# Moving rows of a hybrid decoder step's projections, begun at other bytes modulo 64

## The chip, the cores and the metric

The kernel runs on one NeuronCore of a Trainium2 chip. The metric is the device time of one execution in microseconds. The kernel before was timed twice: 1699.39 and 1699.59 us, median 1699.49 us. A profile of one further execution, and the packed trace of it, are what is read below.

## What is computed

One layer of a decoder, over a prompt of 256 tokens with 16 learned tokens ahead of it, and 8 sample sequences of one token each, 280 token columns in all. Model width 2048, feed-forward width 5632 (up-projection 11264). Cut to what matters:

```
z   = rmsnorm(x) @ w_in                       # 2048 -> 128 strips of 128 features, and 16 for the gates
mix = sigmoid(g_a)*shortconv_branch + sigmoid(g_b)*mlstm_branch
x   = x + mix @ w_out                         # 2048 -> 2048
up  = causal_dwconv(rmsnorm(x) @ w_up)        # 2048 -> 11264
x   = x + (silu(up[5632:]) * up[:5632]) @ w_down   # 5632 -> 2048
y   = rmsnorm(x)[16:]                         # and the states
```

Everything is float32, and the products must keep nearly that precision.

## The kernel before, in words

Tokens lie along the free dimension, features along the 128 partitions. Every large projection is a loop over strips of 128 output features. A strip takes KT = 16 blocks of the contraction (FC = 22 for each half of the last projection), in units of 8 (KU), the last one of 6. For a unit, 8 blocks of weights are fetched by the SP queue into `w_raw` (a ring of RING = 4 slots of 4096 bytes in a partition), ScalarE writes their high part as fp32r to `w_hi` (L712), VectorE the rest to `w_lo` (L985), and TensorE multiplies three times, in `unit`: high weights by the high part of the activations (L1524), high weights by the low part (L1528), low weights by the high part (L1532), 8 matmuls each. Each matmul has a 128x128 stationary operand of its own; the moving operand is one row of an activation tile, 264 to 280 fp32r numbers. All of them run into one PSUM bank, and the next strip goes to the next of four banks.

The activations are held as a high and a low tile:

- `xh`, `xl`: 16 rows of 280 numbers, 1120 bytes from row to row. Strips of the first projection read columns 12 to 279 (268, C0 = 12) or, for three of each head's sixteen, 0 to 279 (280). The sums for the gates (`gates`, L1475) read 280 with a stationary operand of 104 columns.
- `mh`, `ml`: 16 rows, 1088 bytes from row to row (MW = 272), 266 numbers from column MX = 4. Input of the out-projection.
- `x2h`, `x2l`: the same form, in the memory of `xh` and `xl`. Input of the up-projection.
- `hh`, `hl`: 22 rows of 264 numbers, 1056 bytes from row to row, input of the last projection.

The allocation puts `x_parts` (and so `xh` and `xl`) at a multiple of 64 bytes, `x2h`, `x2l`, `mh`, `ml`, `hh` and `hl` at 32 above one, and the three weight rings at multiples of 64. The first number that a matmul reads of a row thus lies, modulo 64 bytes, at

| rows | numbers | before, even/odd row | changed, even/odd row |
|---|---|---|---|
| xh, column 12 on | 268 | 48 / 16 | 56 / 24 |
| xl, column 12 on | 268 | 48 / 16 | 28 / 60 |
| xh, column 0 on | 280 | 0 / 32 | 8 / 40 |
| xl, column 0 on | 280 | 0 / 32 | 44 / 12 |
| mh, ml | 266 | 48, 48 | 56, 52 |
| x2h, x2l | 266 | 48, 48 | 0, 60 |
| hh | 264 | 32 / 0 | 48 / 16 |
| hl | 264 | 32 / 0 | 56 / 24 |

Other fp32r matmuls are untouched. Among them is the state sum of `back` (L1619 to L1622), whose moving rows are 258 numbers of `v_hi` and `v_lo`: the first block's at 32 (`v_hi`) and 0 (`v_lo`), the second block's at 40 and 8, since these rows are 1032 bytes apart, the third block's (`v_hi` alone) at 48.

The tiles are written once each by ScalarE (L731) and VectorE (L1027 for `xl`, L1246 and L1249 for `mh` and `ml`, L1281 and L1284 for `x2h` and `x2l`, L1340 and L1342 for `hh` and `hl`).

What the diff touches, with the lines of the profile:

Of the kernel before, what the change touches and what calls it, by code (L numbers as in the profile page):

```python
# [6 lines left out]
def hybrid_decoder_step(nc, ins, outs, scratch_rows, scratch_v, scratch_q):  # L7
# [10 lines left out]
    f32, f32r = mybir.dt.float32, mybir.dt.float32r  # L18
    ALU, ACT = mybir.AluOpType, mybir.ActivationFunctionType
# [7 lines left out]
    P = 128  # L27
# [9 lines left out]
    KT = D // P  # L37
    FT = DFF // P
    TP = NMETA + SEQ
    NT = TP + NS  # L40
# [4 lines left out]
    NM = NT - M0  # L45
    PM = TP - M0
    NF = NT - NMETA
    MX = 4
    MW = (MX + NM + 7) // 8 * 8
    T2 = TP - 2 * P  # L50
    TL = NT - 2 * P
# [14 lines left out]
    KU = 8  # L66
# [37 lines left out]
    with ctx:  # L104
        def sb(name, shape, dt=f32):
            return ctx.enter_context(nc.sbuf_tensor(name, shape, dt))
# [4 lines left out]

        xres = sb("xres", [P, KT, NT])
        x_parts = (nc.sbuf_base + 31) // 32 * 32
        sb("x_parts", [P, 2 * KT * NT])
        xh = nc.alloc_sbuf_tensor_at("xh", [P, KT, NT], f32r, offset=x_parts)
        xl = nc.alloc_sbuf_tensor_at("xl", [P, KT, NT], f32r, offset=x_parts + KT * NT * 4)
        x2h = nc.alloc_sbuf_tensor_at("x2h", [P, KT, MW], f32r, offset=x_parts + 32)
        x2l = nc.alloc_sbuf_tensor_at("x2l", [P, KT, MW], f32r, offset=x_parts + 32 + KT * NT * 4)
        w_raw = sb("w_raw", [P, RING, KU * P])
        w_hi = sb("w_hi", [P, RING, KU * P], f32r)  # L120
        w_lo = sb("w_lo", [P, RING, KU * P], f32r)
# [25 lines left out]
        def at(name, shape, dt=f32):  # L147
            size = int(np.prod(shape[1:])) * 4
            size = (size + 31) // 32 * 32
            t = nc.alloc_sbuf_tensor_at(name, shape, dt, offset=base + cursor[0])  # L150
            cursor[0] += size
            assert cursor[0] <= REGION, (name, cursor[0])
            return t
# [126 lines left out]
        wfx = at("wfx", [P, WR // Q + 1, Q])  # L280
        hh_end = cursor[0]
        cursor[0] = 0
        hl = at("hl", [P, FC, NF], f32r)
        cursor[0] = hh_b
        hh = at("hh", [P, FC, NF], f32r)
        assert hh_end <= cursor[0]
        yt = at("yt", [P, 2, D])
        cursor[0] = FC * NF * 4
        ys = at("ys", [P, P])
        xs = at("xs", [P, KT, NS])  # L290
        x3 = at("x3", [P, 2, NF])
# [76 lines left out]
        def col(c, j):  # L368
            return vecs[:, bass.ds(c * KT + j, 1)]
# [612 lines left out]
        def _(v):  # L982
# [144 lines left out]
            def back(n):  # L1127
# [6 lines left out]
                for i in range(8, HEAD_U):  # L1134
# [89 lines left out]
                    for jj in range(2):  # L1224
                        j = n * 2 + jj
                        k = i - 12 * jj
                        if k == 12:

                            v.wait_ge(cu_done, j + 1)
                            v.tensor_scalar(cv[:, :], cu[:, 2:NCU], col(5, j), None, ALU.mult).then_inc(conv_step, 1)  # L1230
                            v.wait_ge(conv_step, j * 5 + 1)
                            v.scalar_tensor_tensor(out=cv[:, 0:PM], in0=cu[:, 1:1 + PM], scalar=col(4, j), in1=cv[:, 0:PM],
                                                   op0=ALU.mult, op1=ALU.add).then_inc(conv_step, 1)
                        if k == 13:
                            v.wait_ge(pre_step, 3)
                            v.tensor_tensor(cv[:, PM:NM], cv[:, PM:NM], pre_s[:, bass.ds(j, 1), :].rearrange("p a b -> p (a b)"),
                                            ALU.add).then_inc(conv_step, 1)
                            v.wait_ge(conv_step, j * 5 + 2)
                            v.scalar_tensor_tensor(out=cv[:, 0:PM], in0=cu[:, 0:PM], scalar=col(3, j), in1=cv[:, 0:PM],
                                                   op0=ALU.mult, op1=ALU.add).then_inc(conv_step, 1)  # L1240
                        if k == 14:
                            v.tensor_scalar(cu_last[:, :, bass.ds(j, 1)].rearrange("p t a -> p (t a)"), cu[:, NCU - NLAST:NCU],
                                            1.0, None, ALU.mult).then_inc(conv_step, 1)
                        if (k == 26 and jj == 0) or (k == 19 and jj == 1):
                            v.wait_ge(mixed, j + 1)
                            v.tensor_scalar(mh[:, bass.ds(j, 1), MX:MX + NM].rearrange("p a t -> p (a t)"), mx[:, :], 1.0, None,  # L1246
                                            ALU.mult).then_inc(mix_split, 1)
                            v.wait_ge(mix_split, j * 2 + 1)
                            v.tensor_tensor(ml[:, bass.ds(j, 1), MX:MX + NM].rearrange("p a t -> p (a t)"), mx[:, :],  # L1249
                                            mh[:, bass.ds(j, 1), MX:MX + NM].rearrange("p a t -> p (a t)").bitcast(f32),  # L1250
                                            ALU.subtract).then_inc(mix_split, 1)

            front(0, first=True)
# [5 lines left out]
            def tile_of(t, m, a, b):  # L1259
                return t[:, bass.ds(m, 1), a:b].rearrange("p a t -> p (a t)")  # L1260
# [10 lines left out]
            def out_four(n):  # L1271
                for q in range(4):
                    m = n * 4 + q
                    step(n, 8, U_B, 2 * q)
                    v.wait_ge(unit_used, used(n * 8 + (U_B + 2 * q + 1)))
                    v.wait_ge(sq_done, m + 1)
                    v.wait_ge(x2g_step, m * 2 + 1)
                    v.tensor_tensor(x2s[:, :], bank[q][:, 0:NM], tile_of(xres, m, M0, NT), ALU.add)\
                     .then_inc(evacuated, 1)
                    v.wait_ge(evacuated, out_of(n * 4 + (S_B + q)))  # L1280
                    v.tensor_scalar(tile_of(x2h, m, MX, MX + NM), x2s[:, :], col(1, m), None, ALU.mult).then_inc(x2g_step, 1)  # L1281
                    v.tensor_scalar(tile_of(xres, m, M0, NT), x2s[:, :], 1.0, None, ALU.mult)
                    v.wait_ge(x2g_step, m * 2 + 2)
                    v.scalar_tensor_tensor(out=tile_of(x2l, m, MX, MX + NM), in0=x2s[:, :], scalar=col(1, m),  # L1284
                                           in1=tile_of(x2h, m, MX, MX + NM).bitcast(f32), op0=ALU.mult,
                                           op1=ALU.subtract).then_inc(x2g_step, 1)
                    step(n, 8, U_B, 2 * q + 1)

# [115 lines left out]
        def _(pe):  # L1404
# [107 lines left out]
                turn(aux[2][:, t * P:(t + 1) * P], sc_rows[:, t, :], P)  # L1512
            turn(aux[2][:, 2 * P:2 * P + NS * H], n_rows[:, :], NS * H).then_inc(f_turned, 1)

            def unit(u, slot, b, k0, kk, rh, rl, c0, c1, first, last, waits=(), frees=1):


                pe.wait_ge(hi_done, u + 1)
                for k in range(kk):
                    for at_k, sm, value in waits:  # L1520
                        if at_k == k:
                            pe.wait_ge(sm, value)
                    w = slice(k * P, (k + 1) * P)
                    pe.matmul(bank[b][:, 0:c1 - c0], w_hi[:, slot, w], rh[:, k0 + k, c0:c1],  # L1524
                              start=(first and k == 0), stop=False)
                for k in range(kk):
                    w = slice(k * P, (k + 1) * P)
                    pe.matmul(bank[b][:, 0:c1 - c0], w_hi[:, slot, w], rl[:, k0 + k, c0:c1], start=False, stop=False)  # L1528
                pe.wait_ge(lo_done, u + 1 + RING)
                for k in range(kk):  # L1530
                    w = slice(k * P, (k + 1) * P)
                    mm = pe.matmul(bank[b][:, 0:c1 - c0], w_lo[:, slot, w], rh[:, k0 + k, c0:c1],  # L1532
                                   start=False, stop=(last and k == kk - 1))
                if frees:
                    mm.then_inc(unit_used, frees)

            def strip(s, u, i, b, rh, rl, c0, c1, need=(), between=None):

                for h in range(2):
                    if h == 1 and between is not None:
                        between()
                    waits = [(k - h * KU, sm, x) for k, sm, x in need if k // KU == h]
                    if h == 1:
                        waits.append((2, evacuated, s + 2))
                    unit(u + h, (i + h) % RING, b, h * KU, KU, rh, rl, c0, c1, h == 0, h == 1, waits)

            def tiles_ready(done, per, start, n):

# [92 lines left out]
            back(H - 1)  # L1643

            def out_strip(i, q, need=()):
                strip(i * 4 + (S_B + q), i * 8 + (U_B + 2 * q), 2 * q, q, mh, ml, MX, MX + NM, need)

            def out_unit(q, h, waits, frees):
                unit(U_B + 2 * q + h, 2 * q + h, q, h * KU, KU, mh, ml, MX, MX + NM, h == 0, h == 1, waits, frees)

            out_unit(0, 0, ((0, mix_split, KT),), 1)
            out_unit(1, 0, ((0, evacuated, S_B + 2),), 0)
# [6 lines left out]
                    out_strip(i, q)  # L1659

            def up_strip(c, i, q, need=(), between=None):
                strip(i * 4 + (S_C + c * S_CH + q), i * 8 + (U_C + c * U_CH + 2 * q), 2 * q, q, x2h, x2l, MX, MX + NM, need, between)

            def down_strip(c, i, q, need=(), bank_free=None):

# [96 lines left out]
```

## Time and profile before

| what | value |
|---|---|
| median of two timed executions | 1699.49 us |
| the profiled execution | 1699.21 us |
| its span, first to last instruction | 1697.5 us |
| mean granted TensorE clock | 0.998 |
| TensorE busy with matmuls | 1686.0 us, 99% |
| VectorE, ScalarE, GpSimd busy | 70%, 45%, 28% |
| HBM traffic | 187 GB/s over the span |

A group of matmuls in the profile shows the mean time of one from its start to its end. Matmuls overlap, so that mean (some 285 ns) is not what one costs. What one costs is the distance between starts. In the timeline, a row gives the start of the first of a run of equal instructions and their number; the distance between the starts of two rows, divided by the matmuls between them, is the cost of one.

### The profile page before, as it was taken

How to read it: one execution, taken by the hardware profiler on the slowest of the kernel's cores; microseconds unless marked ns; L12 is line 12 of the kernel's file. 1: busy time of each engine (PE TensorE's matmuls, PEld its weight loads, DVE VectorE, ACT ScalarE, POOL GpSimd, SP SyncE). 2: the span in 40 equal slices, each digit the busy share in tenths (PEclk: the TensorE clock that was granted, in tenths of full speed). 3: DMA queues.
4: the chain of work that ended last, by engine and by line, in shares of the span. 5: the costliest groups of instructions: out<-in, count | busy, mean ns of one | idle time of the engine just before them, and what ended most of it. 6: DMA issues, size and time to landing. Idle time of an engine off the chain costs nothing.

```text
span 1697.5 us, 37171 instructions
## 1 busy us (share of the span) xinstructions
PE 1686.0 (99%) x13712; PEld 1679.5 (99%) x13712; DVE 1193.6 (70%) x1901; ACT 767.4 (45%) x916; POOL 477.9 (28%) x501
## 2 busy tenths in 40 slices
PE   9999999999999999999999999999999999999997
PEld 8999999999999999999999999999999999999997
DVE  5875857677585767758688877777545777777554
ACT  6545345354543535344445554544443433334443
POOL 4522415242241524224333222221000222222220
PEclk9999999999999999999999999999999999999999
DMA  8788786868778687887866666666666666666663
GB/s 212 187 227 196 202 214 166 216 176 216 190 195 213 174 210 178 216 195 190 193 176 187 188 178 180 184 174 178 184 179 183 181 180 177 180 180 177 184 177 120
DMA packets 591309, 318.80 MB, mean 188 GB/s; under 512 B 17756, under 2 KB 586060, under 8 KB 589156
## 3 DMA queue, kind: packets, MB, share of 16 engines
q1 hardware_dynamic: 578564, 292.99, 64.2%
q10 hardware_dynamic: 10592, 21.57, 5.1%
q0 software_dynamic: 2064, 2.92, 0.8%
q8 instruction: 72, 1.18, 0.3%
q14 instruction: 17, 0.14, 0.0%
HBM read 305.09 MB, written 12.78 MB: 187 GB/s over the span
## 4 chain that ended last, share of the span: by engine, by line
PE 99%; ACT 0%; DVE 0%; POOL 0%; issue 0%; ACTq 0%; POOLq 0%; DVEq 0%
PE strip L1524 32%; PE strip L1532 32%; PE strip L1528 32%; PE aux L1406 1%; PE strip L1455 0%; PE aux L1585 0%; PE aux L1414 0%; PE aux L1475 0%; PE strip L1468 0%; PE aux L1615 0%; PE aux L1614 0%; PE aux L1628 0%; PE strip L1406 0%; PE aux L1619 0%; PE aux L1620 0%; PE aux L1612 0%
## 5 line engine op out<-in xcount | busy, mean ns | idle before, releaser
L712 ACT ACTIVATE w_hi<-w_raw 128x1024 fp32r<-128x1024 f32 x557 | 588.7, 1060 | 787.7 <-PE strip L1532 768.8
L985 DVE TENSOR_TENSOR w_lo<-w_raw,w_hi 128x1024 fp32r<-128x1024 f32 x556 | 708.4, 1278 | 297.5 <-ACT w_hi L712 297.0
L1524 PE MATMUL strip<-xh,w_hi 128*128 128x268 f32 (+1 forms) x2016 | 290.9, 286 | 0.0
L1528 PE MATMUL strip<-xl,w_hi 128*128 128x268 f32 (+1 forms) x2016 | 290.0, 286 | 0.0
L1532 PE MATMUL strip<-xh,w_lo 128*128 128x268 f32 (+1 forms) x2016 | 290.0, 286 | 0.0
L1524 PEld LDWEIGHTS strip<-xh,w_hi 128*128 128x128 f32 x2016 | 265.1, 188 | 0.2
L1532 PEld LDWEIGHTS strip<-xh,w_lo 128*128 128x128 f32 x2016 | 265.2, 188 | 0.0
L1528 PEld LDWEIGHTS strip<-xl,w_hi 128*128 128x128 f32 x2016 | 265.2, 188 | 0.0
L1524 PE MATMUL strip<-x2h,w_hi 128*128 128x266 f32 x1408 | 200.1, 284 | 0.0
L1528 PE MATMUL strip<-x2l,w_hi 128*128 128x266 f32 x1408 | 199.9, 284 | 0.0
L1532 PE MATMUL strip<-x2h,w_lo 128*128 128x266 f32 x1408 | 199.8, 284 | 0.0
L1524 PEld LDWEIGHTS strip<-x2h,w_hi 128*128 128x128 f32 x1408 | 183.2, 189 | 0.1
L1532 PEld LDWEIGHTS strip<-x2h,w_lo 128*128 128x128 f32 x1408 | 183.2, 189 | 0.0
L1528 PEld LDWEIGHTS strip<-x2l,w_hi 128*128 128x128 f32 x1408 | 183.2, 189 | 0.0
L683 POOL TENSOR_TENSOR gg<-sg,cz 128x264 f32<-128x264 f32 x44 | 57.9, 1317 | 409.3 <-ACT sg L930 409.3
L686 POOL TENSOR_TENSOR hid<-gg,cz 128x264 f32<-128x264 f32 x44 | 73.7, 1674 | 101.7 <-DVE cz L1334 101.7
L1524 PE MATMUL strip<-hh,w_hi 128*128 128x264 f32 x704 | 102.2, 286 | 0.0
L1532 PE MATMUL strip<-hh,w_lo 128*128 128x264 f32 x704 | 101.3, 285 | 0.0
L1528 PE MATMUL strip<-hl,w_hi 128*128 128x264 f32 x704 | 101.2, 284 | 0.0
L1532 PEld LDWEIGHTS strip<-hh,w_lo 128*128 128x128 f32 x704 | 92.2, 189 | 0.0
L1528 PEld LDWEIGHTS strip<-hl,w_hi 128*128 128x128 f32 x704 | 91.9, 188 | 0.0
L1524 PEld LDWEIGHTS strip<-hh,w_hi 128*128 128x128 f32 x704 | 91.7, 188 | 0.0
(330 smaller groups left out, 1526.4 us busy)
## 6 DMA issues: line engine op xcount, KB each, us to landing
w_raw<-in_w_in SPq DMA_DIRECT2D x256, 512.0 KB, 4.5
w_raw<-in_w_up SPq DMA_DIRECT2D x176, 512.0 KB, 4.1
w_raw<-in_w_down SPq DMA_DIRECT2D x64, 512.0 KB, 3.9
w_raw<-in_w_out SPq DMA_DIRECT2D x32, 512.0 KB, 4.4
w_raw<-in_w_down SPq DMA_DIRECT2D x32, 384.0 KB, 3.3
out<-c_st ACTq DMA_DIRECT2D x8, 1024.0 KB, 7.1
c_st<-in_state_mlstm_C ACTq DMA_DIRECT2D x7, 1024.0 KB, 10.6
rb<-scratch_rows ACTq DMA_DIRECT2D x8, 270.0 KB, 5.3
```

What stands on the lines that cost most here:

```text
L683: g.tensor_tensor(gg[:, :], sg[:, :], cz[:, 0, :], ALU.mult).then_inc(gg_done, 1)
L686: g.tensor_tensor(hid[:, :], gg[:, :], cz[:, 1, :], ALU.mult).then_inc(hid_done, 1)
L712: act.activation(w_hi[:, slot, :], w_raw[:, slot, :], ACT.Copy).then_inc(hi_done, 1)
L985: v.tensor_tensor(w_lo[:, slot, :], w_raw[:, slot, :], w_hi[:, slot, :].bitcast(f32), ALU.subtract).then_inc(lo_done, 1)
L1406: return pe.transpose(out, in_, ident[0:k, 0:k])
L1524: pe.matmul(bank[b][:, 0:c1 - c0], w_hi[:, slot, w], rh[:, k0 + k, c0:c1], start=(first and k == 0), stop=False)
L1528: pe.matmul(bank[b][:, 0:c1 - c0], w_hi[:, slot, w], rl[:, k0 + k, c0:c1], start=False, stop=False)
L1532: mm = pe.matmul(bank[b][:, 0:c1 - c0], w_lo[:, slot, w], rh[:, k0 + k, c0:c1], start=False, stop=(last and k == kk - 1))
```

## The change

Constants for where each tile's rows begin take the place of the common ones. The flat tiles get 8 or 16 numbers more, and a shifted view of the flat tile is the tile. `mh` and `ml` keep their places and are used from column 6 and 5 on in place of 4; `unit` and `strip` get an argument `l0`, the first column in the low tile.

```diff
-    MX = 4
+    MX, MH, ML = 4, 6, 5
+    X2H, X2L, HS, HL, XH, XL = 8, 15, 4, 6, 2, 3
...
-        sb("x_parts", [P, 2 * KT * NT])
-        xh = nc.alloc_sbuf_tensor_at("xh", [P, KT, NT], f32r, offset=x_parts)
-        xl = nc.alloc_sbuf_tensor_at("xl", [P, KT, NT], f32r, offset=x_parts + KT * NT * 4)
-        x2h = nc.alloc_sbuf_tensor_at("x2h", [P, KT, MW], f32r, offset=x_parts + 32)
-        x2l = nc.alloc_sbuf_tensor_at("x2l", [P, KT, MW], f32r, offset=x_parts + 32 + KT * NT * 4)
+        sb("x_parts", [P, 2 * KT * NT + 16])
+        def rows_from(flat, shift, n, width):
+            return flat[:, shift:shift + n * width].rearrange("p (k t) -> p k t", t=width)
+
+        xh = rows_from(nc.alloc_sbuf_tensor_at("xh", [P, KT * NT + 8], f32r, offset=x_parts), XH, KT, NT)
+        xl = rows_from(nc.alloc_sbuf_tensor_at("xl", [P, KT * NT + 8], f32r, offset=x_parts + 32 + KT * NT * 4), XL, KT, NT)
+        x2h_f = nc.alloc_sbuf_tensor_at("x2h", [P, KT * MW + 16], f32r, offset=x_parts + 32)
+        x2l_f = nc.alloc_sbuf_tensor_at("x2l", [P, KT * MW + 16], f32r, offset=x_parts + 64 + KT * NT * 4)
+        x2h, x2l = rows_from(x2h_f, X2H, KT, MW), rows_from(x2l_f, X2L, KT, MW)
...
-        hl = at("hl", [P, FC, NF], f32r)
+        hl = rows_from(at("hl", [P, FC * NF + 8], f32r), HL, FC, NF)
         cursor[0] = hh_b
-        hh = at("hh", [P, FC, NF], f32r)
+        hh = rows_from(at("hh", [P, FC * NF + 8], f32r), HS, FC, NF)
...
-                            v.tensor_scalar(mh[:, bass.ds(j, 1), MX:MX + NM].rearrange("p a t -> p (a t)"), mx[:, :], 1.0, None,
+                            v.tensor_scalar(mh[:, bass.ds(j, 1), MH:MH + NM].rearrange("p a t -> p (a t)"), mx[:, :], 1.0, None,
...
-                    v.tensor_scalar(tile_of(x2h, m, MX, MX + NM), x2s[:, :], col(1, m), None, ALU.mult).then_inc(x2g_step, 1)
+                    v.tensor_scalar(tile_of(x2h, m, 0, NM), x2s[:, :], col(1, m), None, ALU.mult).then_inc(x2g_step, 1)
...
-            def unit(u, slot, b, k0, kk, rh, rl, c0, c1, first, last, waits=(), frees=1):
+            def unit(u, slot, b, k0, kk, rh, rl, c0, c1, first, last, waits=(), frees=1, l0=None):
+                l0 = c0 if l0 is None else l0
+                l1 = l0 + c1 - c0
...
-                    pe.matmul(bank[b][:, 0:c1 - c0], w_hi[:, slot, w], rl[:, k0 + k, c0:c1], start=False, stop=False)
+                    pe.matmul(bank[b][:, 0:c1 - c0], w_hi[:, slot, w], rl[:, k0 + k, l0:l1], start=False, stop=False)
...
-                strip(i * 4 + (S_B + q), i * 8 + (U_B + 2 * q), 2 * q, q, mh, ml, MX, MX + NM, need)
+                strip(i * 4 + (S_B + q), i * 8 + (U_B + 2 * q), 2 * q, q, mh, ml, MH, MH + NM, need, l0=ML)
...
-                strip(i * 4 + (S_C + c * S_CH + q), i * 8 + (U_C + c * U_CH + 2 * q), 2 * q, q, x2h, x2l, MX, MX + NM, need, between)
+                strip(i * 4 + (S_C + c * S_CH + q), i * 8 + (U_C + c * U_CH + 2 * q), 2 * q, q, x2h, x2l, 0, NM, need, between)
```

No instruction is added or removed. `x_parts` is 64 bytes longer, so the weight rings and the small tiles behind it lie 64 bytes later; they stay at multiples of 64 where they were, and the region behind them (`mh`, `ml`, `hl`, `hh`) begins where it did.

## Rows read from the trace of the kernel before

**Rows 1.** The page: busy time, granted clock, the chain that ended last.
```profile
PE 1686.0 (99%) x13712; PEld 1679.5 (99%) x13712; DVE 1193.6 (70%) x1901; ACT 767.4 (45%) x916; POOL 477.9 (28%) x501
...
PEclk9999999999999999999999999999999999999999
...
PE 99%; ACT 0%; DVE 0%; POOL 0%; issue 0%; ACTq 0%; POOLq 0%; DVEq 0%
```
**Rows 2.** Groups by form on TensorE: count, busy us, mean ns, idle before.
```profile
L1528 PE MATMUL strip<-xl,w_hi 128*128 128x268 f32 x1648 | 235.1, 284 | 0.0
...
L1528 PE MATMUL strip<-x2l,w_hi 128*128 128x266 f32 x1408 | 199.9, 284 | 0.0
...
L1528 PE MATMUL strip<-hl,w_hi 128*128 128x264 f32 x704 | 101.2, 284 | 0.0
...
L1528 PE MATMUL strip<-xl,w_hi 128*128 128x280 f32 x368 | 54.9, 291 | 0.0
...
L1528 PE MATMUL strip<-ml,w_hi 128*128 128x266 f32 x256 | 36.3, 284 | 0.0
```
**Rows 3.** Timeline of TensorE, rows of 268: start us, us, what, count.
```profile
655.54 1.14 PE L1528 MATMUL strip<-xl,w_hi 128*128 128x268 f32 x8
...
667.26 1.02 PE L1528 MATMUL strip<-xl,w_hi 128*128 128x268 f32 x7
```
**Rows 4.** Timeline of TensorE, rows of 280.
```profile
635.70 1.20 PE L1528 MATMUL strip<-xl,w_hi 128*128 128x280 f32 x8
...
642.91 1.19 PE L1532 MATMUL strip<-xh,w_lo 128*128 128x280 f32 x8
```
**Rows 5.** Timeline of TensorE, rows of 266, out-projection, then up-projection.
```profile
900.38 1.14 PE L1524 MATMUL strip<-mh,w_hi 128*128 128x266 f32 x8
...
905.25 1.01 PE L1532 MATMUL strip<-mh,w_lo 128*128 128x266 f32 x7
...
1119.84 1.14 PE L1524 MATMUL strip<-x2h,w_hi 128*128 128x266 f32 x8
...
1125.68 0.53 PE L1524 MATMUL strip<-x2h,w_hi 128*128 128x266 f32 x3
```
**Rows 6.** Timeline of TensorE, rows of 264, last projection.
```profile
1255.45 0.89 PE L1524 MATMUL strip<-hh,w_hi 128*128 128x264 f32 x6
...
1265.64 1.13 PE L1524 MATMUL strip<-hh,w_hi 128*128 128x264 f32 x8
```
**Rows 7.** Timeline of TensorE, the state sum of one head, 258 numbers.
```profile
290.19 0.28 PE L1620 MATMUL aux<-v_lo,k_hi 128*128 128x258 f32 x1
290.32 0.28 PE L1621 MATMUL aux<-v_hi,k_lo 128*128 128x258 f32 x1
290.43 0.29 PE L1619 MATMUL aux<-v_hi,k_hi 128*128 128x258 f32 x1
290.56 0.29 PE L1620 MATMUL aux<-v_lo,k_hi 128*128 128x258 f32 x1
290.68 0.28 PE L1621 MATMUL aux<-v_hi,k_lo 128*128 128x258 f32 x1
290.80 0.28 PE L1622 MATMUL aux<-v_hi,k_hi 80*128 80x258 f32 x1
290.92 0.51 PE L1628 MATMUL aux<-sel,sacc 128*128 128x8 f32 x4
```
**Rows 8.** The chain in order of time: the gates' 32 matmuls, start and us.
```profile
27.40 4.14 PE aux L1475 x32
```
**Rows 9.** Timeline of the weight loads, four of them beside matmuls of 8 numbers.
```profile
191.26 0.54 PEld L1628 LDWEIGHTS aux<-sel,sacc 128*128 128x128 f32 x4
191.72 0.19 PEld L1633 LDWEIGHTS aux<-p_hi,ones 128*128 128x128 f32 x1
```
**Rows 10.** What TensorE waited for; then VectorE's writers of moving tiles, by form.
```profile
PE aux L1414 <- POOL a L483: 2.1, 1, 2.1
PE aux L1727 <- DVE rfs L1016: 1.1, 1, 1.1
PE strip L1455 <- DVE xl L1027: 0.6, 2, 0.3
...
L1342 DVE TENSOR_TENSOR hl<-hid,hh 128x264 f32 x44 | 19.1, 433 | 5.4
L1284 DVE SCALAR_TENSOR_TENSOR x2l<-x2s,vecs,x2h 128x266 f32 x16 | 15.6, 972 | 0.0
```

More of the change, by code:

```diff
@@ L282, in hybrid_decoder_step @@
         cursor[0] = 0
-        hl = at("hl", [P, FC, NF], f32r)
+        hl = rows_from(at("hl", [P, FC * NF + 8], f32r), HL, FC, NF)
         cursor[0] = hh_b
-        hh = at("hh", [P, FC, NF], f32r)
+        hh = rows_from(at("hh", [P, FC * NF + 8], f32r), HS, FC, NF)
         assert hh_end <= cursor[0]
         yt = at("yt", [P, 2, D])
-        cursor[0] = FC * NF * 4
+        cursor[0] = FC * NF * 4 + 32
         ys = at("ys", [P, P])
@@ L1245, in back @@
                             v.wait_ge(mixed, j + 1)
-                            v.tensor_scalar(mh[:, bass.ds(j, 1), MX:MX + NM].rearrange("p a t -> p (a t)"), mx[:, :], 1.0, None,
+                            v.tensor_scalar(mh[:, bass.ds(j, 1), MH:MH + NM].rearrange("p a t -> p (a t)"), mx[:, :], 1.0, None,
                                             ALU.mult).then_inc(mix_split, 1)
                             v.wait_ge(mix_split, j * 2 + 1)
-                            v.tensor_tensor(ml[:, bass.ds(j, 1), MX:MX + NM].rearrange("p a t -> p (a t)"), mx[:, :],
-                                            mh[:, bass.ds(j, 1), MX:MX + NM].rearrange("p a t -> p (a t)").bitcast(f32),
+                            v.tensor_tensor(ml[:, bass.ds(j, 1), ML:ML + NM].rearrange("p a t -> p (a t)"), mx[:, :],
+                                            mh[:, bass.ds(j, 1), MH:MH + NM].rearrange("p a t -> p (a t)").bitcast(f32),
                                             ALU.subtract).then_inc(mix_split, 1)
@@ L1280, in out_four @@
                     v.wait_ge(evacuated, out_of(n * 4 + (S_B + q)))
-                    v.tensor_scalar(tile_of(x2h, m, MX, MX + NM), x2s[:, :], col(1, m), None, ALU.mult).then_inc(x2g_step, 1)
+                    v.tensor_scalar(tile_of(x2h, m, 0, NM), x2s[:, :], col(1, m), None, ALU.mult).then_inc(x2g_step, 1)
                     v.tensor_scalar(tile_of(xres, m, M0, NT), x2s[:, :], 1.0, None, ALU.mult)
                     v.wait_ge(x2g_step, m * 2 + 2)
-                    v.scalar_tensor_tensor(out=tile_of(x2l, m, MX, MX + NM), in0=x2s[:, :], scalar=col(1, m),
-                                           in1=tile_of(x2h, m, MX, MX + NM).bitcast(f32), op0=ALU.mult,
+                    v.scalar_tensor_tensor(out=tile_of(x2l, m, 0, NM), in0=x2s[:, :], scalar=col(1, m),
+                                           in1=tile_of(x2h, m, 0, NM).bitcast(f32), op0=ALU.mult,
                                            op1=ALU.subtract).then_inc(x2g_step, 1)
@@ L1535, in unit, with strip @@
                     mm.then_inc(unit_used, frees)
-            def strip(s, u, i, b, rh, rl, c0, c1, need=(), between=None):
+            def strip(s, u, i, b, rh, rl, c0, c1, need=(), between=None, l0=None):
                 for h in range(2):
@@ L1546, in strip @@
                         waits.append((2, evacuated, s + 2))
-                    unit(u + h, (i + h) % RING, b, h * KU, KU, rh, rl, c0, c1, h == 0, h == 1, waits)
+                    unit(u + h, (i + h) % RING, b, h * KU, KU, rh, rl, c0, c1, h == 0, h == 1, waits, l0=l0)
             def tiles_ready(done, per, start, n):
@@ L1645, in out_strip @@
             def out_strip(i, q, need=()):
-                strip(i * 4 + (S_B + q), i * 8 + (U_B + 2 * q), 2 * q, q, mh, ml, MX, MX + NM, need)
+                strip(i * 4 + (S_B + q), i * 8 + (U_B + 2 * q), 2 * q, q, mh, ml, MH, MH + NM, need, l0=ML)
             def out_unit(q, h, waits, frees):
-                unit(U_B + 2 * q + h, 2 * q + h, q, h * KU, KU, mh, ml, MX, MX + NM, h == 0, h == 1, waits, frees)
+                unit(U_B + 2 * q + h, 2 * q + h, q, h * KU, KU, mh, ml, MH, MH + NM, h == 0, h == 1, waits, frees, ML)
             out_unit(0, 0, ((0, mix_split, KT),), 1)
```

## The prediction

> **What bounds the kernel now.** I read the page first, then TensorE's groups by form, its waits, and last the timeline of one stretch for each length of row. The page settles the engine: TensorE is busy 99% of the span, the chain that ended last is TensorE for 99% of its length, and the clock is full in all slices [rows 1]. The waits leave nothing for another engine to give back: TensorE waited 2.1 + 1.1 + 0.6 = 3.8 us in three places [rows 10]. So the time is the number of matmuls times the distance between their starts, and the change can only act on that distance.
>
> The counts are in the groups. Each form has three groups of the same count (L1524, L1528, L1532), one of which is shown [rows 2]: 3 x 1648 = 4944 matmuls of 268 numbers, 3 x 368 = 1104 of 280, 3 x 256 = 768 and 3 x 1408 = 4224 of 266, 3 x 704 = 2112 of 264, together 13152. The mean of 284 to 291 ns in these rows is not the cost. The cost comes from the timeline:
>
> - 268: 96 matmuls from 655.54 to 667.26, 11.72/96 = 122.1 ns [rows 3]
> - 280: 56 from 635.70 to 642.91, 7.21/56 = 128.8 ns [rows 4]
> - 266: 40 from 900.38 to 905.25, 121.8 ns, and 48 from 1119.84 to 1125.68, 121.7 ns [rows 5]
> - 264: 84 from 1255.45 to 1265.64, 10.19/84 = 121.3 ns [rows 6]
>
> Sum: 603.6 + 142.1 + 93.5 + 513.9 + 256.2 = 1609.3 us of the 1697.5 us of the span. The other 88.2 us (first and last strips' edges, transposes, score and state sums, start and tail) the change hardly touches.
>
> At the full clock (2.4 GHz) one number takes 0.417 ns. What a matmul costs beyond its numbers is then 122.1 - 111.7 = 10.4 ns for 268, 128.8 - 116.7 = 12.1 ns for 280, 10.9 ns for 266 and 121.3 - 110.0 = 11.3 ns for 264. This excess, some 25 to 29 clocks, is what a different first byte could change. It is 142 us of the time in all (13152 x 10.8 ns).
>
> **The change part by part.** Nothing is added or removed, and nothing moves in the order of instructions or DMAs. Three parts remain.
>
> First, TensorE's moving rows begin elsewhere. What the trace says of the first byte is little. Rows at 48/16 have an excess of 10.4 ns, at 48 alone 10.9, at 32/0 11.3, at 0/32 with 280 numbers 12.1 [rows 3 to 6]. All of these are multiples of 16 bytes, and between the least and the most lie 1.7 ns. The length differs along with the byte, so the byte may have no part in it. If all rows came down to the least of these, the gain would be 1104 x 1.7 + 4992 x 0.5 + 2112 x 0.9 = 1.9 + 2.5 + 1.9 = 6.3 us; if the differences are due to length, it is nothing. I take half, 3 us, as the value: the byte moves away from 0/32 where the excess is highest, but no row shows 52, 56 or 60. The three places before that are read at 48 (out- and up-projection) are already close to the least, so they can give little by this reckoning.
>
> Both ends of the unknown cost, from the nearest rows. Below: weight loads beside matmuls of only 8 numbers come every (191.72 - 191.26)/4 = 115 ns [rows 9], and no fp32r matmul with a load of its own can be expected below that; at 115 ns for all, 1609.3 - 13152 x 0.115 = 97 us would go. Above: the one place where moving rows begin off a multiple of 16 is the state sum. The starts of its first block (bytes 0 and 32) go from 290.19 to 290.43, 120 ns a matmul; those of its second (40, 8, 40) from 290.43 to 290.80, 123.3 ns [rows 7], 3.3 ns more. The same two numbers stand in the other heads to 10 ns. But starts scatter by 2 to 3 ns around their grid, and all six from 290.19 to 290.92 average 121.7 ns, the same as rows of 266. So 3.3 ns is an upper bound and about half of it a fair reading.
>
> Second, the writers. VectorE and ScalarE write the tiles at other bytes, in the same number of instructions of the same length. I take nothing. The cover: VectorE is idle 30% of the span, ScalarE 55% [rows 1], and the writers are 44 + 44 instructions of some 300 to 430 ns and 16 + 16 of up to 972 ns [rows 10]. If each of the about 230 writers became half as slow again, the added time would be some 50 us spread over 1697 us of an engine with 500 us to spare. Only where TensorE begins a stage with a tile just written would it be seen, at four stage borders of under 0.5 us each; the first of these is the 0.6 us of L1455 on `xl`.
>
> Third, the rings of weights lie 64 bytes later, at multiples of 64 as before. The same weight columns are thus read from other places relative to the moving rows. Nothing in the trace shows a cost of this; 266-number rows take four different places modulo 256 in turn and every 8 of them take the same time (0.97 us) [rows 5]. I take nothing, bounds inside those of the first part.
>
> The sum: profiled execution 1699.21 us, less 3 us, 1696.2; the median of the timed runs is 0.3 us above the profiled one, so **1696.5 us**.
>
> **A rule of the Trainium skill that speaks against the change.** The page "SBUF — State Buffer", section "Specifications (TRN2)", says that SBUF is read in lines of 16 bytes, that two hits in a line are needed for full bandwidth, and that a move to a new line costs. By that rule a row that begins at 60 meets its first line with one number only, and a row of 268 from 56, 24, 28 or 60 touches 68 lines, from 48 or 16 only 67. Its section "Operand start alignment" states the legality of such starts and says that nothing was timed. What the rule would do here, as a mechanism, is the first rival's smaller price.
>
> **Rivals.**
>
> *Slower: a start off a multiple of 16 costs.* Place: every matmul whose row no longer begins at a multiple of 16, that is all of `xh` and `xl` (6048), `x2l` (1408), `mh` and `ml` (768), `hl` (704), 8928 in all; `x2h` and `hh` stay at multiples. Price: the 3.3 ns of [rows 7] give 29.5 us, 1729; half of it, 1714. A second way to a price: one line more is four numbers more, at the slope from 268 to 280 (6.7 ns/12 = 0.56 ns a number) [rows 3, 4] 2.2 ns, for `xh`, `xl`, `x2l` and `hl`, which get a line more (8160), 18 us, 1717.5. I take 1718. For it: the only unaligned rows of the trace look dearer. Against: the average of 121.7 over all six. It decides from about 0.4 ns a matmul on, where it outweighs the 3 us.
>
> *Clearly faster: the first byte sets part of the excess, and the end of a 64-byte piece is its best place.* For it: 280 numbers at 0/32 are dearer by 1.7 ns than 268 at 48/16 after the numbers are taken off, which may be the byte. If another such step comes with 52 to 60, all matmuls gain it: 13152 x 1.7 = 22 us, 1677. Against: 264 numbers at 32/0 differ by 0.9 ns only, and 266 and 258 numbers take the same 121.7 ns at very different bytes. Over 2% (34 us) needs 2.6 ns on every matmul, a quarter of the excess.
>
> *Nothing at all.* Rows of 258, 264 and 266 numbers all take 121.3 to 121.8 ns, though 8 numbers are 3.3 ns. That looks like a floor of another kind, the cycle of loading the next weights while one matmul runs. Then the byte doesn't matter below 268 numbers, and the time is 1699 us. Against a floor by the load: the gates' matmuls, with 104 columns in place of 128 to load, take 4.14/32 = 129.4 ns [rows 8], as much as the strips' 280 with 128; but there the numbers themselves may bind.
>
> The page "TensorE: Matmul & The Clock Gate", section "LDWEIGHTS (loading the stationary operand)", puts a load at its columns over 1.2 GHz, 106.7 ns for 128; the trace's 115 ns is near that, and by this rule only some 15 ns would be left between load and distance, with the first byte acting on no more than that.
>
> **How the numbers follow.** Small gain as forecast (1692 to 1699): 0.40. Nothing (1699 to 1701): 0.15. Slower by the start: 0.25, of which 0.05 is over 1733. Clearly faster: 0.20, of which 0.07 is below 1665.5. The range for 8 in 10 leaves 0.1 on either side: 1674 (somewhat below the faster rival's 1677) to 1726 (just under the upper price of the slower one). A difference of under 2% is about what a measurement of this kernel can't tell from no change, and by these cases: faster by over 2% 0.07, within 2% 0.88, slower by over 2% 0.05.
>
> **What would show it.** The profile after should have the same counts, TensorE at 99% of the chain, and no new wait of TensorE. The forecast is right if the distance between starts in the same stretches is 121.2 to 122.1 ns for 264 to 268 numbers and 127.5 to 128.5 ns for 280. The slower rival shows as 123.5 to 125 ns in `xh`, `xl`, and as a difference between L1524 and L1528 in the up-projection, since `x2h` begins at 0 and `x2l` at 60. The faster one shows as 120 ns or less in all. It would prove me wrong on the writers if L1342 or L1284 were much longer and TensorE waited for them, and wrong on the rings if the state sum, whose rows don't move, changed its 121.7 ns.

## The result, and the profile after

The changed kernel takes 1720.12 us (1719.39 and 1720.86) against 1699.49 us: slower by 1.2%, ratio 1.0119, 95% interval 1.0102 to 1.0135. The forecast was 1696.5 us, a small gain. The time lies inside the range, on the other side of the forecast, beside the rival priced at 1718 us.

The page of the changed kernel has the same counts, the same clock and the same bound as before [rows 1]: TensorE with 99% of the chain.

```profile
span 1717.7 us, 37171 instructions
...
PE 1706.2 (99%) x13712; PEld 1700.0 (99%) x13712; DVE 1195.6 (70%) x1901; ACT 767.6 (45%) x916; POOL 478.2 (28%) x501
...
PEclk9999999999999999999999999999999999999999
...
PE 99%; ACT 0%; DVE 0%; POOL 0%; issue 0%; ACTq 0%; POOLq 0%; DVEq 0%
```

TensorE's waits, and the writers of the low tiles, hardly moved against [rows 10], so neither a wait nor a slower writer took the 20 us:

```profile
PE aux L1419 <- POOL a L488: 2.1, 1, 2.1
PE aux L1734 <- DVE rfs L1021: 1.1, 1, 1.1
PE strip L1460 <- DVE xl L1032: 0.6, 2, 0.3
...
L1347 DVE TENSOR_TENSOR hl<-hid,hh 128x264 f32 x44 | 19.1, 435 | 6.3
L1289 DVE SCALAR_TENSOR_TENSOR x2l<-x2s,vecs,x2h 128x266 f32 x16 | 15.1, 944 | 0.0
```

What is left is the distance between starts. The timeline of TensorE in the changed kernel, first rows of 268 numbers, then the up-projection's 266, then the last projection's 264 (columns: start us, us, what, count):

```profile
665.50 1.16 PE L1531 MATMUL strip<-xh,w_hi 128*128 128x268 f32 x8
666.50 1.15 PE L1535 MATMUL strip<-xl,w_hi 128*128 128x268 f32 x8
667.48 1.16 PE L1539 MATMUL strip<-xh,w_lo 128*128 128x268 f32 x8
668.48 1.16 PE L1531 MATMUL strip<-xh,w_hi 128*128 128x268 f32 x8
...
1121.51 1.15 PE L1531 MATMUL strip<-x2h,w_hi 128*128 128x266 f32 x8
1122.50 1.15 PE L1535 MATMUL strip<-x2l,w_hi 128*128 128x266 f32 x8
1123.49 1.14 PE L1539 MATMUL strip<-x2h,w_lo 128*128 128x266 f32 x8
1124.46 1.15 PE L1531 MATMUL strip<-x2h,w_hi 128*128 128x266 f32 x8
...
1270.59 0.90 PE L1531 MATMUL strip<-hh,w_hi 128*128 128x264 f32 x6
...
1278.70 0.90 PE L1531 MATMUL strip<-hh,w_hi 128*128 128x264 f32 x6
```

From the starts: 24 matmuls of x in 2.98 us, 124.2 ns where it was 122.1 [rows 3]; 24 of the up-projection in 2.95 us, 122.9 for 121.7 [rows 5]; 66 of the last projection in 8.11 us, 122.9 for 121.3 [rows 6].

The same over the whole trace, adding up the distance from each matmul's start to the next one's: `xh`, `xl` +11.1 us, of which 9.6 with 268 numbers and 1.5 with 280; up-projection +5.9; last projection +3.2; out-projection +0.7; everything else -0.7; together 20.2 us, which is the difference of the spans (1717.7 - 1697.5).

For what follows, cycles of 2.4 GHz per matmul are the finer unit: the distance from a group's first start to the next group's first start, by 8 (or 6), times 2.4, its mean over all such groups, those with a wait in them or right behind a transpose left out. The kernel before has 293.5 for x, 292.0 for out- and up-projection, 291.3 for the last one (the mean of its three kinds). Runs with the same addresses in a stage agree to 0.3 or better. In the changed kernel:

| rows | with w_hi, high | with w_hi, low | with w_lo, high |
|---|---|---|---|
| x, 268 (56/24; 28/60) | 300.2 | 295.6 | 298.6 |
| x, 280 (8/40; 44/12), 309.0 before | 313.2 | 308.5 | 313.6 |
| out-projection (56; 52) | 292.1 | 297.4 | 292.8 |
| up-projection (0; 60) | 296.0 | 297.0 | 293.1 |
| last projection (48/16; 56/24) | 294.3 | 298.7 | 292.3 |

Two things in it fit no theory of the prediction. `x2h` at 0, a multiple of 16, costs 4 cycles more with `w_hi` and 1 with `w_lo`, though the rows are the same. And `mh` at 56 costs next to nothing (0.1 and 0.8), although 56 is no multiple of 16.

### The profile page after: what moved, and what is told of

Read it like the earlier page. It is cut to its first block, busy times and chain, and to the rows that moved or that the text cites. A ratio compares the mean times of both kernels' runs of the same rounds, so it can differ in the third digit from the quotient of the medians.

```text
span 1717.7 us, 37171 instructions
## 1 busy us (share of the span) xinstructions
PE 1706.2 (99%) x13712; PEld 1700.0 (99%) x13712; DVE 1195.6 (70%) x1901; ACT 767.6 (45%) x916; POOL 478.2 (28%) x501
## 4 chain that ended last, share of the span: by engine, by line
PE 99%; ACT 0%; DVE 0%; POOL 0%; issue 0%; ACTq 0%; POOLq 0%; DVEq 0%
PE strip L1531 32%; PE strip L1535 32%; PE strip L1539 32%; PE aux L1411 1%; PE strip L1460 0%; PE aux L1592 0%; PE aux L1419 0%; PE aux L1480 0%; PE strip L1473 0%; PE aux L1622 0%; PE aux L1621 0%; PE aux L1635 0%; PE strip L1411 0%; PE aux L1628 0%; PE aux L1627 0%; PE aux L1626 0%
## 5 line engine op out<-in xcount | busy, mean ns | idle before, releaser
L1531 PE MATMUL strip<-xh,w_hi 128*128 128x268 f32 (+1 forms) x2016 | 295.9, 289 | 0.0
L1539 PE MATMUL strip<-xh,w_lo 128*128 128x268 f32 (+1 forms) x2016 | 293.9, 288 | 0.0
L1531 PEld LDWEIGHTS strip<-xh,w_hi 128*128 128x128 f32 x2016 | 270.3, 190 | 0.2
L1539 PEld LDWEIGHTS strip<-xh,w_lo 128*128 128x128 f32 x2016 | 269.1, 189 | 0.0
```

## The experiments

Four theories were set against each other. A: the moving row's own first byte sets the cost. B: the 64 bytes by which the weight rings moved. C: that high and low rows no longer lie a multiple of 256 bytes apart. D, after the first two rounds: the distance from the weights to the moving row.

### Rings alone, starts alone

The first kernel is the one before with

```diff
-        sb("x_parts", [P, 2 * KT * NT])
+        sb("x_parts", [P, 2 * KT * NT + 16])
```

> The kernel before with x_parts 16 numbers longer and nothing else: the weight rings lie 64 bytes later as in the changed kernel, every moving row begins where it did before. Theory A (the first byte of the moving row sets the cost): 1699.5 us, distances of 122.1, 121.7 and 121.3 ns as before. Theory B (the place of the weights relative to the moving rows sets it): the whole loss, 1720 us. A mixture would lie between, and its share can be read off.

Measured: 1699.98 us, ratio 1.0001 (0.9989 to 1.0012). The second is the changed kernel with `vecs` and `scale_t` allocated ahead of `w_raw`, which brings the rings back modulo 512:

```diff
+        vecs = sb("vecs", [P, 6 * KT + CW * 2 * FT])
+        scale_t = sb("scale_t", [P, NS])
         w_raw = sb("w_raw", [P, RING, KU * P])
```

> The changed kernel, its rings put back modulo 512 to where they were before (vecs and scale_t, 1472 bytes, are allocated ahead of them). Theory A: 1720 us as the changed kernel. Theory B: 1699.5 us.

Measured: 1725.47 us, ratio 1.0149 (1.0120 to 1.0179). B falls: with the old rows the rings' 64 bytes cost nothing in the total, and the rows' places alone cost the whole loss. Inside the total the rings do move something: in the kernel with the rings alone the last projection's `hh` with `w_hi` goes from 290.2 to 293.5 cycles and `hh` with `w_lo` from 292.1 to 291.2, 0.6 us for that stage over its trace. And the two don't add up. With the rings back the loss is 5 us larger than in the changed kernel, whose rings happen to lie better for its rows. The two intervals touch, so it is the groups that show this (the out-projection's `mh` with `w_lo` is at 296.9 cycles here and 292.8 there, `xh` with `w_lo` at 301.0 and 298.6). So the place of the weights does have a part, once the rows have moved.

### The x rows alone, all rows but x

> Rings as before modulo 512, xh and xl at the changed kernel's bytes (56/24 and 28/60), all other rows at the old ones. Theory A, from the distances in the changed kernel (xh with w_hi +2.9 ns, with w_lo +2.3 ns, xl +1.0 ns on 1648 matmuls each, about +2 ns on 736 of those with 280 numbers): about +12 us, 1711.5. Theory B: 1699.5 us.

```diff
-    MX, MH, ML = 4, 6, 5
-    X2H, X2L, HS, HL, XH, XL = 8, 15, 4, 6, 2, 3
+    MX, MH, ML = 4, 4, 4
+    X2H, X2L, HS, HL, XH, XL = 4, 12, 0, 0, 2, 3
```

Measured: 1718.17 us, ratio 1.0106 (1.0077 to 1.0136).

> Rings as before modulo 512, xh and xl at the old bytes (48/16), mh, ml, x2h, x2l, hh, hl at the changed kernel's. Theory A: about +9 to +10 us, 1709, of which 6 in the up-projection, 3 in the last projection and 0.7 in the out-projection. Theory B: 1699.5 us.

```diff
-    X2H, X2L, HS, HL, XH, XL = 8, 15, 4, 6, 2, 3
+    X2H, X2L, HS, HL, XH, XL = 8, 15, 4, 6, 0, 8
```

Measured: 1712.74 us, ratio 1.0075 (1.0045 to 1.0104).

Both were over what A gave, by 6.7 and 3.7 us. One reason is that A's figures came from the changed kernel, whose rings lie elsewhere (above). The other, 4.7 us of the first and 1.8 us of the second, stands in rows that I had meant to leave alone. To put the low tile back at its old byte modulo 64, these two kernels leave it 64 bytes further than before from its high tile. In the run with x rows alone the up-projection, at 48 and 48, shows 292.0 / 296.5 / 295.5 cycles (high, low, high with `w_lo`) for 292.0 in all three before, 4.7 us. In the other, x at 48/16 shows 295.5 / 294.2 / 293.5, 1.8 us with the rows of 280. The first byte modulo 64 is thus not the whole of it, and C became a theory.

### High and low at one phase again, and at two

Three kernels put each low tile a multiple of 64 from its high one: the first two at a distance from it that is as before modulo 256, the third with the low tile 64 bytes later. Of the changed kernel the first two alter the two offsets (`x_parts + KT * NT * 4` for `xl` and `x_parts + 32 + KT * NT * 4` for `x2l`, rings back as above) and the constants:

```diff
-    MX, MH, ML = 4, 6, 5
-    X2H, X2L, HS, HL, XH, XL = 8, 15, 4, 6, 2, 3
+    MX, MH, ML = 4, 5, 5
+    X2H, X2L, HS, HL, XH, XL = 7, 7, 5, 5, 2, 2
```

> High and low rows begin at the same byte modulo 256 again, as in the kernel before, but at new bytes: x at 56/24, out-projection 52, up-projection 60, last projection 52/20; rings as before. Theory A (a row that begins off a multiple of 16, or at another byte modulo 64, costs by itself): at least the changed kernel's loss, 1720 us or more, in all three groups of a unit alike. Theory C (each byte is as good as another; what costs is that the low rows no longer follow the high ones at a distance of a multiple of 256, so that the regular step from row to row breaks at each change between high and low): 1699.5 us, 121.7 ns in the up-projection.

Measured: 1739.45 us, ratio 1.0230 (1.0200 to 1.0259), the slowest but one of all.

```diff
+    MX, MH, ML = 4, 6, 6
+    X2H, X2L, HS, HL, XH, XL = 8, 8, 8, 8, 4, 4
```

> As the one before, at other bytes: x at 0/32, out-projection 56, up-projection 0, last projection 0/32 (high and low alike). Theory A in its form of multiples of 16: 1699.5 but for the out-projection; in its form of a byte modulo 64, some 4 cycles a matmul in the up-projection (x2h cost that at 0), 1707. Theory C: 1699.5 us.

Measured: 1717.33 us, ratio 1.0100 (1.0070 to 1.0129), ten microseconds over A's 1707: x at 0/32, for which A gave no price, costs 4.5 cycles more than at 48/16.

The third has both offsets 64 bytes later than these, and `ml` and `hl` too:

```diff
+    MX, MH, ML = 4, 4, 4
+    X2H, X2L, HS, HL, XH, XL = 4, 4, 0, 0, 0, 0
...
+        cursor[0] += 64
         ml = at("ml", [P, KT, MW], f32r)
...
-        cursor[0] = 0
+        cursor[0] = 64
         hl = rows_from(at("hl", [P, FC * NF + 8], f32r), HL, FC, NF)
```

> Every row begins at its old byte modulo 64 (48/16, 48, 48, 32/0), but each low tile lies 64 bytes further from its high tile, so that their distance is 64 modulo 256 and no longer a multiple. Theory A: 1699.5 us. Theory C: a loss like that seen on the up-projection of the run with x rows alone (x2l +4.5, x2h with w_lo +3.6 cycles a matmul, x2h with w_hi nothing), so about 2.7 cycles or 1.1 ns on the mean of 13152, 14 us, 1713.

Measured: 1705.37 us, ratio 1.0034 (1.0022 to 1.0046).

C as the main cause falls with the first of the three: one phase throughout, and the largest loss. In the first two of these runs the three kinds of group in a unit agree to 0.3 cycles for rows of 266 and 268 (the last projection's don't; between `hh` and `hl` the distance is no multiple of 256): 294.0 at 56, 296.0 at 0, 300.0 at 52 for 266 numbers. So a place has a price of its own. C's effect is real but small: 5.7 us for all low tiles 64 bytes off, where 14 were expected, and the up-projection's cycles are to the tenth those of the run with x rows alone.

Where that small part arises can be seen matmul by matmul. In the run with x rows alone the eight distances of `x2h` with `w_hi` are 125, 121, 122, 118, 125, 121, 122, 118 ns or near it, a pattern of four rows. With `w_lo`, behind the shifted `x2l`, they are 123, 128, 122, 125 and then 125, 121, 122, 118. It takes four matmuls to fall back into the pattern, and they cost some 12 ns together.

The last of this round keeps the high rows and moves the low ones by a single number:

```diff
+    MX, MH, ML = 4, 4, 5
+    X2H, X2L, HS, HL, XH, XL = 4, 5, 0, 1, 0, 1
```

> High rows at their old bytes, low rows 4 bytes later (52/20, 52, 52, 36/4). Theory A: the low groups (L1535) alone cost more, the high ones (L1531, L1539) are as before. Theory C: groups behind a change between high and low cost more, L1539 too, whose rows lie where they lay; by how much at 4 bytes is open, 0 to 14 us.

Measured: 1725.37 us, ratio 1.0147 (1.0117 to 1.0176). The timeline of the up-projection in this kernel:

```profile
1120.44 1.14 PE L1531 MATMUL strip<-x2h,w_hi 128*128 128x266 f32 x8
1121.41 1.18 PE L1535 MATMUL strip<-x2l,w_hi 128*128 128x266 f32 x8
1122.43 1.14 PE L1539 MATMUL strip<-x2h,w_lo 128*128 128x266 f32 x8
1123.40 1.14 PE L1531 MATMUL strip<-x2h,w_hi 128*128 128x266 f32 x8
```

The high groups take 0.97 to 0.98 us as before, the low one between them 1.02 us, 5% more. Over the trace `x2l` is at 305.5 cycles and `x2h` at 292.0 and 292.5. For x the low rows stand at 305.6, the unmoved high ones at 297.6 and 296.2 for 293.5. Both theories have their part here, A the larger one: 4 bytes on the low tiles alone cost 26 us, more than the whole change. The out-projection's `ml` at the same 52 shows only 294.0, against 300.0 where `mh` lies at 52 too. So a group's price also depends on what ran before it.

### Other multiples of 16, and 8 and 4 past them

```diff
+    MX, MH, ML = 4, 0, 0
+    X2H, X2L, HS, HL, XH, XL = 12, 12, 4, 4, 8, 8
```

> High and low rows alike, all at multiples of 16 that the kernel before doesn't use: x at 16/48 (280 numbers: 32/0), out-projection 32, up-projection 16, last projection 48/16. Theory A (the byte modulo 16 costs, multiples of 16 are cheap; at 0 the rows of 266 and 268 cost 4 cycles more than at 48): 1699 to 1712 us; no group over 298 cycles. If some multiple of 16 is better than 48, its group falls under 291 cycles.

Measured: 1708.22 us, ratio 1.0047 (1.0027 to 1.0066), inside A's range; no group came under 291 cycles in its mean.

```diff
+    MX, MH, ML = 4, 2, 2
+    X2H, X2L, HS, HL, XH, XL = 0, 0, 2, 2, 1, 1
```

> High and low rows alike: up-projection at 32 (a multiple of 16), out-projection at 40, last projection 40/8 (8 past one), x at 52/20 (4 past one). Theory A, with what the earlier runs gave for 4 or 12 past a multiple of 16 (6 to 13 cycles a matmul) and 8 past (2 to 7): up-projection 292 to 296 cycles, out-projection 294 to 299, last projection 294 to 299, x 300 to 305 (280 numbers 314 to 320): 1715 to 1735 us.

Measured: 1740.77 us, ratio 1.0233 (1.0203 to 1.0263), 6 us over A's range; x, at the upper end of what A gave for it or above (305.6 and 319.8 cycles), takes 30 of the 41 us. The same-phase runs together, cycles per matmul by first byte modulo 64, weights at a multiple of 64:

| numbers | multiple of 16 | 8 past one | 4 or 12 past one |
|---|---|---|---|
| 266 | 48: 292.0; 32: 294.0; 0: 296.0; 16: 296.0 | 56: 294.0; 40: 293.5 to 297.0 | 52: 300.0; 60: 298.0 |
| 268 | 48/16: 293.5; 16/48: 293.3; 0/32: 298.0 | 56/24: 300.1 | 52/20: 305.6 |
| 280 | 0/32: 309.0; 32/0: 309.0; 16/48: 309.9 | 8/40: 313.9 | 4/36: 319.8 |
| 264 | 32/0: 291.3; 0/32: 291.7; 48/16: 292.6 | 40/8: 299.1 | 52/20: 303.4 |

A multiple of 4 that is none of 8 costs 6 to 12 cycles, one of 8 that is none of 16 costs 2 to 8, and within the multiples of 16 there are 4 to 5 cycles between the best and the worst. No place beat the kernel before by more than 0.2 cycles. The 298.0 at 60 is no steady value but the mean of two, 296.1 and 300.0 (last section).

The Trainium skill, page "SBUF — State Buffer", section "Specifications (TRN2)", would count lines of 16 bytes. A row of 266 touches 67 of them from 0, 16, 32, 48, 52 and 56 alike, and these six cost 292 to 300 cycles here; from 60 it touches 68, and costs 298.0, less than from 52. Rows of 268 do cost more where they touch a line more (300.1 at 56/24 for 293.5 at 48/16). So the count of lines agrees with some of these traces and doesn't predict the price.

### Moving the weights, not the rows

The kernel before again, with the rings 32 bytes later:

```diff
-        sb("x_parts", [P, 2 * KT * NT])
+        sb("x_parts", [P, 2 * KT * NT + 8])
```

> The kernel before with its rings of weights 32 bytes later (x_parts 8 numbers longer), so that the distance from the weights to the moving rows changes modulo 64 and no moving row does. Theory A (the moving row's own byte): 1699.5 us. Theory D (the distance between the moving row's byte and the weights' modulo 64): rows at 48 act as rows at 16, those of 268 as at 16/48, and the groups' cycles are those of the run with 16 and 32 in place of 292 and 293, by up to 4 cycles, 5 to 15 us.

Measured: 1714.23 us, ratio 1.0077 (1.0048 to 1.0106). No moving row lies elsewhere (the small tiles behind the rings move along with them), and seven tenths of the change's loss are there (14.2 of 20.6 us). The up-projection over 120 us in the middle of the span (columns: stretch, its length, PE busy and matmuls, clock, DMA share, GB/s), first the kernel before:

```profile
1040.00:1160.00 120.00, 120.00 (x989) 1.00 0.63 180
```

then the kernel with the rings 32 bytes later:

```profile
1040.00:1160.00 120.00, 120.00 (x975) 1.00 0.61 175
```

and the last kernel, rings and rows both 32 bytes later (x, up- and last projection; the out-projection's rows stay):

```profile
1040.00:1160.00 120.00, 120.00 (x989) 1.00 0.62 180
```

with

```diff
-        sb("x_parts", [P, 2 * KT * NT + 16])
+        sb("x_parts", [P, 2 * KT * NT + 8])
...
+    MX, MH, ML = 4, 4, 4
+    X2H, X2L, HS, HL, XH, XL = 12, 12, 8, 8, 8, 8
```

> Rings 32 bytes later as in the run before this one, and x, up-projection and last projection's rows 32 bytes later as well (16/48, 16, 0/32), so that the distance between rows and weights is that of the kernel before; the out-projection's rows stay at 48, as a control that must show 296 cycles again. Theory D (the distance modulo 64 decides): up-projection back to 292 cycles, x to 293, last projection to 290, about 1701 us. Theory E (weights at 32 modulo 64 cost some 4 cycles by themselves, and the rows' own byte is a second, separate cost): the up-projection 296 or more, x 298 or so, 1714 us or more.

Measured: 1704.45 us, ratio 1.0028 (1.0017 to 1.0040). In full (cycles, mean of the three kinds, or the three kinds):

| | before | rings +32 | rings and rows +32 |
|---|---|---|---|
| up-projection | 292.0 | 296.0 | 292.0 |
| last projection | 290.2, 291.5, 292.1 | 295.1, 293.9, 292.9 | 290.2, 291.4, 292.1 |
| x, 268 | 293.5 | 295.9 | 295.4 |
| out-projection (rows not moved) | 292.0 | 296.0 | 296.0 |

In the up-projection, 16 with the weights at 32 costs 292, 16 with the weights at 0 costs 296, 48 with the weights at 32 costs 296, and 48 with the weights at 0 costs 292. There the distance decides, not the byte. In the last projection, too, each kind came back to 0.1 cycle when rows and weights moved together. E (weights at 32 dear by themselves) falls, since the up-projection came back in full. The control stayed at 296.0.

D in its form modulo 64 holds for the rows of 266 alone, and for them only while high and low rows lie a multiple of 256 apart (with `x2l` 64 bytes later it costs 296.5, at the same distance modulo 64). It said that with the rings 32 bytes later x would cost what it costs at 16/48 with the weights at a multiple of 64, 293.3 cycles; it cost 295.9. The last projection at 32/0 with the rings 32 later and at 0/32 with the rings in place has the same distance modulo 64, and costs 295.1 / 293.9 / 292.9 in the one and 291.5 / 290.8 / 292.9 in the other (high, low, high with `w_lo`). The distances of these pairs differ by 64 bytes. All this is for shifts of 32 and 64 bytes. No run moved the weights by 4 or 8, so whether the dearer places off a multiple of 16, which make most of the change's loss, are a matter of the row's own byte or of its distance to the weights is not shown.

For x the mean came back only in small part (3.8 of 4.7 us stayed). The trace says what differs. The timeline of the last kernel in one head, before and after the head's middle, where TensorE does the state sums between two strips:

```profile
253.87 1.16 PE L1535 MATMUL strip<-xl,w_hi 128*128 128x268 f32 x8
254.87 1.15 PE L1539 MATMUL strip<-xh,w_lo 128*128 128x268 f32 x8
255.86 1.16 PE L1531 MATMUL strip<-xh,w_hi 128*128 128x268 f32 x8
256.85 1.16 PE L1535 MATMUL strip<-xl,w_hi 128*128 128x268 f32 x8
...
296.52 1.14 PE L1539 MATMUL strip<-xh,w_lo 128*128 128x268 f32 x8
297.49 1.14 PE L1531 MATMUL strip<-xh,w_hi 128*128 128x268 f32 x8
298.47 1.14 PE L1535 MATMUL strip<-xl,w_hi 128*128 128x268 f32 x8
299.45 1.14 PE L1539 MATMUL strip<-xh,w_lo 128*128 128x268 f32 x8
```

The same rows of the same tiles, with weights from the same ring, take 2.98 us for 24 matmuls in the one stretch and 2.93 in the other: 993 ns for eight, or 976. Both values are in the kernel before too, 993 and 994 in about a tenth of the groups of 268 and 975 to 978 in most others; in the last kernel the dear one holds over two fifths, in seven of the eight heads from the strips of 280 to the state sums, and behind the state sums in one group at most. So the levels came back with the distance, and the share of each did not.

## Why the prediction was wrong

*What bounds the kernel.* Right: TensorE, the distance between its starts, and nothing else. Counts, stages and the sum of 1609 us stood, and the 20.2 us are found in the terms that the sum named, save for -0.7.

*The first part, "I take half, 3 us, as the value: the byte moves away from 0/32 where the excess is highest".* This is the step that failed, in its sign. It took half of what the differences among four aligned places could give as a gain, and entered nothing for what the new bytes, which no row had shown, could cost. The bytes before were the cheap ones. Rows of 280 went from 309.0 cycles to 313.2, 308.5 and 313.6 when they left 0/32, and at the other aligned places tried, 32/0 and 16/48, they cost 309.0 and 309.9, so leaving 0/32 had nothing to give; 48/16 was not tried for them. Rows of 268 went from 293.5 to 300.2, 295.6 and 298.6. In the place of the 3 us gained stand +11.1 us for x and +5.9, +3.2 and +0.7 for the others.

*The upper bound was the better reading.* It was so by luck of size. The 3.3 ns of the state sum [rows 7] are what 4 past a multiple of 16 costs (8 cycles for 266 numbers at 52), but they came from starts at 8 past one, for which the same-phase runs show 2 to 8 cycles. And they weren't a price of the byte: over the eight heads the second block is dearer than the first by 2.8 ns in the kernel before, 1.9 in the changed one and 5.8 with the rings alone moved, with the same rows at the same bytes.

*The slower rival, 1718 us.* Its time was right and its place half right. It counted `xh`, `xl`, `x2l`, `mh`, `ml` and `hl` and left out `x2h` and `hh` as multiples of 16. In the changed kernel `x2h` alone costs 3.0 us and `hh` 1.0, while `mh`, counted, costs 0.1. So the sign it gave, a difference between the up-projection's groups, is only 1 cycle (296.0 and 297.0). The places among the multiples of 16 differ by up to 4 cycles, which the kernel before could not show for rows of 266, all at 48 with the weights at a multiple of 64. The 18 us were from the slope of 0.56 ns a number; that it met the total is partly chance.

*"Nothing at all", a floor.* Wrong in what it concluded: rows of 264 to 266 numbers take from 289 to 306 cycles in the means of these runs, so the byte matters below 268 numbers. Whether something else holds all of them above 289 cycles is open; no run tested it.

*The second part, the writers: nothing.* Right [rows 10]; L1289 even fell from 972 to 944 ns.

*The third part, the rings: nothing.* Right for the 64 bytes with the rows at their old places (ratio 1.0001), wrong as a rule: with the new rows the same 64 bytes are worth 5 us, and 32 bytes with the old rows cost 14.2. The argument for it, that every 8 rows take the same time at four places modulo 256, shows only that the pattern of four repeats. The sign that the prediction set itself, a state sum that leaves its 121.7 ns though its rows don't move, did appear. The same six distances in the changed kernel:

```profile
293.02 0.28 PE L1627 MATMUL aux<-v_lo,k_hi 128*128 128x258 f32 x1
...
293.76 0.51 PE L1635 MATMUL aux<-sel,sacc 128*128 128x8 f32 x4
```

Over the trace the six take 735 or 736 ns in every head, 122.6 each, where they took 725 to 731. The rings by themselves don't do this: with the rings alone moved the six take 724 or 725.

The Trainium skill, page "TensorE: Matmul & The Clock Gate", section "Step-by-step: what each phase is for", says that weights have a read port of their own, so that loading them steals nothing from the running matmul. The kernel with the rings 32 bytes later speaks against it: of the matmuls' operands only the weights lie elsewhere, the instructions are the same, and eight matmuls take 987 ns in place of 973. That the same weights cost 973 again once the rows followed shows that their place alone is not it.

## What to carry to other kernels

Where TensorE is the bound and each matmul has a stationary operand of its own, keep moving rows in 4-byte types at multiples of 16 bytes: off them a matmul cost up to 14 cycles more in 292. Among the multiples of 16 the distance from rows to weights is worth a sweep, up to some 5 cycles here. Weights off a multiple of 32 were not tried. Compare places by the distance between starts in a profile, group by group, and not by the total, since the total mixes places that gain and lose. And a change that only lengthens a tile ahead of the weights can cost 0.8% without touching a line of the loop.

## What the runs showed of the hardware that was not expected

- The cost of a matmul depends on the distance from its moving row to the weights, and for shifts of 32 bytes that distance decided (292.0 against 296.0 cycles for rows of 266, both ways round). Taken modulo 64 it is not enough for rows of 264 and 268.
- It has memory. Equal groups settle on one of several levels and hold it: 976 or 993 ns for eight rows of 268 in the last kernel. In the same-phase run with `x2h` at 60 the eight rows take 987 ns in the first half of the up-projection and 1000 in the second, at the same addresses. The state sums, whose operands no run moved, take 724, 731 or 736 ns for six matmuls in different kernels. The two stretches of 120 us in the run with `x2h` at 60:

```profile
1040.00:1160.00 120.00, 120.00 (x975) 1.00 0.62 179
1420.00:1540.00 120.00, 120.00 (x962) 1.00 0.60 175
```

- What picks the level is open. The entry into a stage seems to, since it changes behind the state sums in the last kernel and between the two halves of the up-projection with `x2h` at 60, but no run forced it. Also open is how the distance acts above 64 bytes: 64 bytes on the rings leave 266 numbers at 292.0 and turn the 976 ns of x into a mixture of 970 and 983, with no change of the mean. That two reads of SBUF collide is a reading of the distance's effect; no counter in the trace shows a collision.
